# Expert gates: who compares which keys, on VectorE and GpSimd

## The reference, cut to what matters

```
experts = e1 * N_KEYS + e2          # N_KEYS = 128, 16384 experts
g = jax.nn.softmax(cs, axis=-1)
...
act = jax.nn.gelu(jnp.einsum('td,tkd->tk', xt, u_tab[et])) * gt
return jnp.einsum('tk,tkd->td', act, v_tab[et])
```

## Time and profile before

| | us |
|---|---|
| median of 3 runs | 2557.13 |
| lowest and highest of them | 2556.34, 2559.05 |
| the profiled execution | 2554.61 |
| its span, first to last instruction | 2552.8 |
| the gate stage in it, from VectorE's first comparison to ScalarE's last copy | 1709.06 to 1816.97 |

### The profile page before, as it was taken

One profiled execution on the slowest core, in us unless ns is written; L12 is line 12 of the kernel. 1 busy time (PEld: TensorE's weight loads), 2 busy tenths in 40 slices (PEclk: granted clock), 3 DMA queues, 4 the chain that ended last, 5 costly groups with the idle time before them and its releaser, 6 DMA issues.

```text
span 2552.8 us, 35383 instructions
## 1 busy us (share of the span) xinstructions
PE 2300.8 (90%) x12530; PEld 1872.7 (73%) x12530; DVE 1417.8 (56%) x2637; ACT 849.5 (33%) x1233; POOL 239.5 (9%) x267
## 2 busy tenths in 40 slices
PE   5899899999979998999899979526799999999998
PEld 1655478878767557998775858425799999999997
DVE  2555253432289354653375433988666666666665
ACT  2333132222253333433133201115544444444443
POOL 0033000000031240000000000029400000000000
PEclk7999999999989999999998989759999999999999
DMA  7237222222252344545332413200255555555553
GB/s 265 66 135 261 83 82 97 92 89 92 91 145 75 116 159 135 184 168 188 127 132 73 142 58 124 75 0 0 91 189 182 189 188 183 188 188 187 187 185 123
DMA packets 92828, 340.46 MB, mean 133 GB/s; under 512 B 10409, under 2 KB 10436, under 8 KB 92496
## 3 DMA queue, kind: packets, MB, share of 16 engines
q1 hardware_dynamic: 89280, 325.10, 37.8%
q0 software_dynamic: 3472, 14.35, 1.8%
HBM read 338.35 MB, written 1.05 MB: 133 GB/s over the span
## 4 chain that ended last, share of the span: by engine, by line
PE 79%; DVE 12%; POOL 4%; ACT 2%; issue 1%; DMA 1%; POOLq 0%; DVEq 0%; SPq 0%; ACTq 0%
PE bank L704 19%; PE bank L934 14%; PE bank L946 14%; PE bank L494 11%; PE bank L731 7%; POOL tail_zone L1902 3%; PE bank L533 3%; DVE main_zone L1316 2%; DVE main_zone L1319 2%; PE bank L675 2%; PE bank L656 2%; PE bank L807 1%; PE bank L664 1%; PE bank L560 1%; DVE first_w_parts L1319 1%
## 5 line engine op out<-in xcount | busy, mean ns | idle before, releaser
L704 PE MATMUL bank<-act_parts,first_w_parts 128*128 128x512 f32 (+1 forms) x2928 | 560.5, 353 | 35.7 <-DVE act_parts L1316 35.2
L704 PEld LDWEIGHTS bank<-act_parts,first_w_parts 128*128 128x128 f32 x2928 | 474.5, 193 | 119.2 <-issue 36.6
L934 PEld LDWEIGHTS bank<-n_parts,w_parts 128*128 128x128 f32 x3072 | 387.2, 193 | 13.6 <-issue 3.9
L934 PE MATMUL bank<-n_parts,w_parts 128*128 128x256 f32 x3072 | 390.3, 284 | 3.7 <-DVE w_parts L1319 3.7
L1319 DVE TENSOR_TENSOR first_w_parts<-weight_ring,first_w_parts 128x1024 fp32r<-128x1024 f32 x166 | 211.3, 1275 | 304.3 <-ACT first_w_parts L1083 303.9
L1319 DVE TENSOR_TENSOR w_parts<-weight_ring,w_parts 128x1024 fp32r<-128x1024 f32 x256 | 312.3, 1221 | 118.2 <-ACT w_parts L1083 118.2
L494 PE MATMUL bank<-main_zone,weight_ring 128*128 128x272 f32 (+2 forms) x1472 | 365.2, 409 | 12.8 <-DVE main_zone L1316 10.0
L946 PE MATMUL bank<-w_parts,a_parts 128*128 128x512 f32 x1536 | 372.7, 392 | 0.5 <-DVE w_parts L1319 0.5
L494 PEld LDWEIGHTS bank<-main_zone,weight_ring 128*128 128x128 f32 x1472 | 282.1, 192 | 90.0 <-issue 43.4
L1083 ACT ACTIVATE w_parts<-weight_ring 128x1024 fp32r<-128x1024 f32 x256 | 269.8, 1055 | 191.6 <-PE bank L934 191.2
L946 PEld LDWEIGHTS bank<-w_parts,a_parts 128*128 128x128 f32 x1536 | 280.5, 189 | 53.7 <-issue 1.1
(11 more groups left out here) (199 smaller groups left out, 1899.4 us busy)
## 6 DMA issues: line engine op xcount, KB each, us to landing
weight_ring<-in_stream SPq DMA_DIRECT2D x618, 512.0 KB, 3.3
main_zone<-in_rel_bias POOLq DMA_DIRECT2D x6, 512.0 KB, 14.2
main_zone<-in_decay POOLq DMA_DIRECT2D x1, 1536.0 KB, 9.2
main_zone<-in_xT POOLq DMA_DIRECT2D x1, 1024.0 KB, 11.5
main_zone<-in_ctxT POOLq DMA_DIRECT2D x1, 1024.0 KB, 16.0
tail_zone<-in_rel_bias POOLq DMA_DIRECT2D x2, 512.0 KB, 24.9
tail_zone<-in_keysT POOLq DMA_DIRECT2D x1, 1024.0 KB, 5.2
out<-main_zone SPq DMA_DIRECT2D x2, 512.0 KB, 2.7
```

Of the source, the lines that this page charges most:

```text
L704: mm = pe.matmul(o[:, 0:w], wb[:, hw, k, :], fin[:, hx, k, 0:w], start=(k == 0 and n == 0), stop=(k == DC - 1 and n == 2))
L934: mm = pe.matmul(bank[e % 3][:, 0:L], w[:, hw, k, :], n2p[:, hx, k, :], start=(k == 0 and n == 0), stop=(k == DC - 1 and n == 2))
```

## The change

A half's work is dealt out anew. VectorE compares all eight second keys of a half in one instruction, 128x1024 in place of 128x512, and makes only the first five of the eight weighted first rows (`OWN1 = 5`). GpSimd makes no second rows any more, and the remaining three first rows, each in one TENSOR_SCALAR with two operations (is_equal, then mult) and two per-token operands, key and weight. It therefore stages two sets of three numbers in place of one set of four: two copies for each half. The counts of TensorE's waits follow; their number and their order do not change.

```
-OWN2 = 4
+OWN1 = 5
@@ TensorE, before each group of four tokens
-                    pe.wait_ge(oh1, at(4 * g + 4, 16))
+                    pe.wait_ge(oh1, at(g // 2 * OWN1 + (OWN1 if g % 2 else 4), 2 * OWN1))
                     pe.wait_ge(oh2, at(g // 2 + 1, 2))
                     if g % 2:
-                        pe.wait_ge(oh2_pool, at(g // 2 + 1, 2))
+                        pe.wait_ge(oh1_pool, at(g // 2 + 1, 2))
@@ VectorE
-                    tt_(one2[:, 8 * g:8 * g + OWN2, :], col(e2, 8 * g, OWN2).unsqueeze(2).broadcast_to([P, OWN2, P]),
-                        iota.unsqueeze(1).broadcast_to([P, OWN2, P]), ALU.is_equal).then_inc(oh2, 1)
-                    for j in range(8 * g, 8 * g + 8):
+                    tt_(one2[:, 8 * g:8 * g + 8, :], col(e2, 8 * g, 8).unsqueeze(2).broadcast_to([P, 8, P]),
+                        iota.unsqueeze(1).broadcast_to([P, 8, P]), ALU.is_equal).then_inc(oh2, 1)
+                    for j in range(8 * g, 8 * g + OWN1):
                         ts(one1[:, j, :], iota, col(e1, j), col(gt, j), ALU.is_equal, ALU.mult).then_inc(oh1, 1)
@@ GpSimd
-            def stage(slot, cols):
-
-                pool.tensor_copy(staged[:, slot], cols).then_inc(e2_staged, 1)
-
-            def second_rows(g):
-                for j in range(8 - OWN2):
-                    last = pool.tensor_scalar(one2[:, 8 * g + OWN2 + j], iota, staged[:, g, j:j + 1], None, ALU.is_equal)
-                last.then_inc(oh2_pool, 1)
+            def stage(slot, j, i=None):
+
+                for n, at in enumerate((E1T0, GT0)):
+                    v = view(at, L + 16)
+                    last = pool.tensor_copy(staged[:, slot, n], v[:, j:j + 8 - OWN1] if i is None
+                                            else v[:, bass.ds(i * 16 + j, 8 - OWN1)])
+                last.then_inc(keys_staged, 1)
+
+            def first_rows(g):
+                for n in range(8 - OWN1):
+                    last = pool.tensor_scalar(one1[:, 8 * g + OWN1 + n, :], iota, staged[:, g, 0, n:n + 1],
+                                              staged[:, g, 1, n:n + 1], ALU.is_equal, ALU.mult)
+                last.then_inc(oh1_pool, 1)
```

More of the change, by code:

```diff
@@ L326, in build @@
         oh2 = sem("second_one_hot_ready")
-        e2_staged = sem("second_keys_staged")
+        keys_staged = sem("first_keys_staged")
         gate_psum = sem("expert_gates_summed")
@@ L331, in build @@
         seeded = sem("residual_in_sum")
-        oh2_pool = sem("second_one_hot_of_gpsimd")
+        oh1_pool = sem("first_one_hot_of_gpsimd")
         n2_split = sem("expert_input_split")
@@ L1891, in _ @@
             pool.wait_ge(seeded, 1)
-            one2 = view(OH20, 16, P)
-            staged = view(ST0, 2, 8 - OWN2)
-            ahead = view(E2T0, L + 8)
-            def stage(slot, cols):
-                pool.tensor_copy(staged[:, slot], cols).then_inc(e2_staged, 1)
-            def second_rows(g):
-                for j in range(8 - OWN2):
-                    last = pool.tensor_scalar(one2[:, 8 * g + OWN2 + j], iota, staged[:, g, j:j + 1], None, ALU.is_equal)
-                last.then_inc(oh2_pool, 1)
-            stage(0, ahead[:, OWN2:8])
+            one1 = view(OH10, 16, P)
+            staged = view(ST0, 2, 2, 8 - OWN1)
+            def stage(slot, j, i=None):
[9 more added lines that the diff above has]
+                last.then_inc(oh1_pool, 1)
+            stage(0, OWN1)
             for g in range(2):
-                pool.wait_ge(e2_staged, g + 1)
+                pool.wait_ge(keys_staged, g + 1)
                 if g:
-                    pool.wait_ge(oh2_pool, g)
-                stage(1 - g, ahead[:, 8 * g + 8 + OWN2:8 * g + 16])
-                second_rows(g)
+                    pool.wait_ge(oh1_pool, g)
+                stage(1 - g, 8 * g + 8 + OWN1)
+                first_rows(g)
             with pool.Fori(1, L // 16) as i:
@@ L1914, in _ @@
                     pool.wait_ge(gate_psum, i * 4 + (2 * g - 2))
[L1915 to L1918, removed]
+                    pool.wait_ge(keys_staged, i * 2 + (g + 1))
+                    pool.wait_ge(oh1_pool, i * 2 + g)
+                    stage(1 - g, 8 * g + 8 + OWN1, i)
+                    first_rows(g)
             pool.wait_ge(ea_ready, KEYS)
```

## The result

The changed kernel takes 2569.7 us (median of 5 runs, 2566.5 to 2573.1), against 2557.1 for the kernel before. The ratio is 1.0051, with a 95% interval from 1.0035 to 1.0067. The forecast was 2556.0 and no measurable difference. So it is slower by half a per cent: outside what was forecast as likeliest, between that case and the rival "held twice".

The account below looks back on a forecast made before the run. GpSimd was taken to set the gate stage's pace: 29 halves at 3.22 for 3.27 us give -1.5, the last half -0.4, the start +0.8, sum -1.1, so 2557.13 becomes 2556.0 us; range 2552 to 2585.

Parts of the forecast that it names:

- held twice: Rival: GpSimd's second operation is held too, the third runs in full behind it; 2572 to 2591 us, chance 0.27.
- the loop of three engines: Gate stage: GpSimd's end releases TensorE, then VectorE's comparison, which holds GpSimd; 3.27 us a half before, 3.22 after.
- the third operation held: GpSimd's third operation makes no progress during VectorE's two-input comparison and ends 0.47 us after it.
- VectorE's relief: VectorE loses three first rows of about 0.28 us each a half; off the path, since it waits for TensorE.
- the wider comparison: VectorE's comparison at 128x1024 takes 1.22 us in place of 0.69, on the loop: +0.53 a half.
- the fourth operation: GpSimd's last operation of each half is gone: -0.58 us a half.
- the second copy: GpSimd's added copy, 0.16 to 0.24 us, lies within the held operation's wait and costs nothing.
- The start: Before the loop: longer hold of GpSimd's first copy and two more copies; -0.3 to +1.4 us, taken as +0.8.
- d: Addition to GpSimd's instruction for two operations and two operands: 0 to 0.32 us, taken as 0, up to 0.12 nearly as likely.
- The edge: Lead of GpSimd's second operation over VectorE's comparison, 0.31 - d us: free at 0.20, held at 0.04, unknown between.
- VectorE held: Rival: VectorE's comparison waits 0.29 us for the rest of GpSimd's second operation; 3.51 a half, 2564 us, chance 0.06.

Follow-up runs that it names:

- one_op: Changed kernel with GpSimd's three first rows made by a comparison alone, without the weight multiplication: 2556.5 us, ratio 0.9996 to the kernel before.
- imm_mult: Changed kernel with a constant 1.0 in place of the per-token weight as GpSimd's second operand: 2564.1 us, ratio 1.0027 to the kernel before.
- after_again: The changed kernel run once more, unaltered, beside the kernel before: 2570.6 us, ratio 1.0059.
- one_copy: Changed kernel with keys and weights staged in one GpSimd copy in place of two: 2568.2 us, ratio 1.0048 to the kernel before.
- own6: Changed kernel with six first rows on VectorE and two on GpSimd (OWN1 = 6): 2538.8 us, ratio 0.9921 to the kernel before.
- extra_copy: Changed kernel with a third copy that nobody reads ahead of GpSimd's operations: 2579.9 us, ratio 1.0095 to the kernel before.
- no_lock: Changed kernel with VectorE's two-input comparison of eight keys replaced by eight comparisons with one key each: 2561.4 us, ratio 1.0015 to the kernel before.

## Why the prediction was wrong

**What bounds the stage**: right. GpSimd through the loop of three engines, VectorE idle before its comparison, the third operation held: all of it is in the trace after, and one_op gives the forecast's half within 0.03 us.

**VectorE's relief is worth nothing, the wider comparison +0.53, the fourth operation -0.58, the second copy nothing in itself**: right, by one_op. The start came out at +0.85 for +0.8, in part by luck: the 0.8 was picked from a wide range, and six dearer instructions were not in it. (VectorE's own work, 1.14 + 5 x 0.28, is 2.54 and not 2.6 us; nothing hangs on it.)

**The step that failed is GpSimd's TENSOR_SCALAR with two operations, d.** It was bounded at 0 to 0.32 us, and I took 0, with up to 0.12 as likely, because a comparison and a multiplication cost the same when alone. It measured 0.19. That two operations cost the same one at a time doesn't say that both in one instruction do: the second adds 0.11 (imm_mult) and its per-token operand 0.08. I had argued from the operation alone, and the edit also added an operand.

**A second term was missed.** "In the loop only the held one's d counts: 3.22 + d" gives 3.41 for the measured d. The half is 3.66. By the terms: the comparison is stretched by 0.10 to 0.13, since it meets, as I read it, a GpSimd instruction still reading; the third ends 0.76 after it and not 0.47 + 0.19 = 0.66; and a few halves are held twice. With 1.55 us to the comparison this is 1.55 + 1.33 + 0.76 = 3.64 for a half that isn't held twice. The prediction's edge was drawn as two states, free or held. In between there is a third in which the GpSimd instruction goes through and VectorE pays.

**The edge** was placed rightly otherwise: in the two executions of the changed kernel the operation mostly got through at leads of 0.17 to 0.20 (0.31 - d would have given 0.12), and at 0.08 to 0.10 it was held in five cases and got through in two. Held twice was no steady state but a part of the halves, and "VectorE held" happened in a mild form, 0.1 us and not the 0.29 of the rival. The predicted time lay 13.7 us too low. That the range held the result is no merit of the mechanism: it reached up for "held twice", and that rival's 2572 with small d lies near the measured 2569.7 by chance, since most halves were not held twice.

**Open:** why a held instruction with a second operand needs 0.10 us more after the comparison's end than an undisturbed one would have left (0.76 for 0.66), and what decides at leads around 0.1: the operation with the constant (imm_mult) got through at all 25 leads of 0.06 to 0.09, where the one with weights was mostly held. And two operations of 1.92 us, in after_again and one_copy, were held with a lead of 0.20. In both cases VectorE came to its comparison straight from its first rows, beside which GpSimd's instruction is itself 0.08 longer (0.87 for 0.79 in own6), so that a lead of 0.20 may have counted as some 0.12; that is argued, and no run tests it.

## What to carry to other kernels

Where two engines are near full, look for the loop of waits first: here VectorE's work was off the path, and giving it less while giving GpSimd dearer instructions could only lose. A wait that is released by the held engine itself fixes where the next collision falls. An instruction less on the held engine (own6) opened the loop and took 28 us off the changed kernel's stage, where one copy less within the loop (one_copy) took 2 to 4. An instruction whose form a trace doesn't show should be priced with a margin for its operands too, and its price carried through each place in the loop where it meets another engine.

## What the runs showed of the hardware

- GpSimd's TENSOR_SCALAR on 128x128 float32: 0.60 us with one operation and one per-partition operand, 0.71 with a second operation on a constant, 0.79 with a second per-partition operand.
- VectorE's two-input comparison against a GpSimd instruction that reads the same memory: GpSimd's ends 0.47, 0.58 or 0.76 us after the comparison's end, by these three forms, when it started after it (in the third form 0.06 us or more after it; nearer to it, 0.58 to 0.67: after_again, extra_copy). When GpSimd started first and was not held, the comparison reads, it seems, from 0.21 to 0.22 us (first two forms) or 0.29 to 0.30 (third) after GpSimd's start; it is longer by what is missing to that.
- Starting first does not always protect GpSimd's instruction: with one operation it was held at leads of 0.04 (before, one_op; it ended 0.40 us past the comparison's end), with two per-token operands in five of seven cases at 0.08 to 0.10 (it ended 0.50 past it; after, after_again), with the constant in none of 25 at 0.06 to 0.09.
- VectorE's TENSOR_SCALARs, close together, stretch a GpSimd instruction of 0.79 us: mostly to 0.86 to 1.03 (no_lock), to 0.87 (own6).
